# Sums of squares of three heads and of one norm as two fp32r matmuls; one table set for the last two heads' factors

## The reference

```
def rmsnorm(x, gain):
    y = x * rsqrt(mean(x * x, axis=-1) + 1e-6)
    return y * gain

o = rmsnorm(o, out_gain)            # per head, over its 128 values
o = o * silu(g)
return o.reshape(B, S, H * V) @ w_out
```

```
x = x + (silu(g) * u) @ w_down
gate = sigmoid(rmsnorm(x, g_ple) @ w_ple_gate)
x = x + gate * (p_i @ w_ple)
```

## Time and profile before

| | us |
|---|---|
| median of 3 runs | 2105.17 |
| lowest, highest | 2104.57, 2105.2 |
| the profiled execution, its own time | 2104.74 |
| its span in the trace | 2102.3 |
| PE busy | 2092.1 |
| POOL busy | 1143.1 |
| DVE busy | 1008.4 |
| ACT busy | 742.9 |

### The profile page before, as it was taken

How to read it: one execution, slowest core, us unless ns; L and a number is a source line. 1 busy time by engine, 2 the same in 40 slices (tenths; PEclk the granted TensorE clock), 3 DMA queues, 4 the chain that set the end, 5 groups by cost and what they waited for, 6 DMA issues and landing times.

```text
span 2102.3 us, 28240 instructions
## 1 busy us (share of the span) xinstructions
PE 2092.1 (100%) x11210; PEld 1738.5 (83%) x11210; DVE 1008.4 (48%) x1184; ACT 742.9 (35%) x862; POOL 1143.1 (54%) x821
## 2 busy tenths in 40 slices
PE   9999999999999999999999999999999999999998
PEld 8888888888888888888888888888888888888887
DVE  6357555555123265634555333744477544453126
ACT  6335542222224445533222233515433332212234
POOL 6677455555555333365555555544566555555553
PEclk9999999999999999999999999999999999999999
DMA  5212132222232222242222222322222222223321
GB/s 199 81 62 82 41 120 100 85 95 100 100 119 96 96 67 94 81 138 95 88 98 100 100 100 100 102 98 101 99 88 94 99 100 100 100 88 105 117 100 60
DMA packets 33209, 204.39 MB, mean 97 GB/s; under 512 B 3688, under 2 KB 6504, under 8 KB 9456
## 3 DMA queue, kind: packets, MB, share of 16 engines
q1 hardware_dynamic: 32896, 203.13, 28.1%
q10 hardware_dynamic: 240, 0.23, 0.0%
HBM read 200.19 MB, written 2.10 MB: 96 GB/s over the span
## 4 chain that ended last, share of the span: by engine, by line
PE 58%; DVE 1%; ACT 1%; issue 0%; DVEq 0%; ACTq 0%
PE bank L1952 58%; DVE x L1835 0%; DVE sgate L1884 0%; ACT w_hi L775 0%; DVE h L1885 0%; PE bank L2363 0%; DVE ssq L1909 0%; ACT sgate L775 0%; DVE h L1931 0%; ACT un L775 0%; ACT L1289 0%; ACT L1286 0%; ACT L1282 0%; ACT L1279 0%; ACT sq L775 0%
## 5 line engine op out<-in xcount | busy, mean ns | idle before, releaser
L652 POOL TENSOR_TENSOR w_lo<-raw,w_hi 128x512 fp32r<-128x512 f32 x676 | 976.6, 1475 | 862.2 <-ACT w_hi L775 862.2
L1952 PE MATMUL bank<-u_hi,w_hi 128*128 128x512 f32 (+1 forms) x1936 | 753.5, 390 | 0.1
L1952 PE MATMUL bank<-u_lo,w_hi 128*128 128x512 f32 (+1 forms) x1936 | 749.4, 387 | 0.0
L775 ACT ACTIVATE w_hi<-raw 128x2048 fp32r<-128x2048 f32 x185 | 354.3, 1915 | 931.4 <-PE bank L1952 927.8
L1952 PE MATMUL bank<-u_hi,w_lo 128*128 128x512 f32 (+1 forms) x1936 | 482.1, 387 | 0.0
L1952 PEld LDWEIGHTS bank<-u_hi,w_hi 128*128 128x128 f32 x1936 | 363.6, 188 | 74.6 <-ACTq L1185 0.5
L1952 PEld LDWEIGHTS bank<-u_lo,w_hi 128*128 128x128 f32 x1936 | 363.7, 188 | 73.7 <-issue 0.2
L1952 PEld LDWEIGHTS bank<-u_hi,w_lo 128*128 128x128 f32 x1936 | 362.5, 188 | 74.6
L1952 PE MATMUL bank<-act_hi,w_hi 128*128 128x512 f32 x528 | 205.4, 389 | 0.0
L1952 PE MATMUL bank<-act_lo,w_hi 128*128 128x512 f32 x528 | 205.4, 389 | 0.0
L1324 DVE TENSOR_TENSOR h<-h,bank 128x512 f32<-128x512 f32 x48 | 30.8, 683 | 300.3 <-PE bank L1952 300.3
(11 more groups left out here) (293 smaller groups left out, 2105.5 us busy)
## 6 DMA issues: line engine op xcount, KB each, us to landing
raw<-wall SPq DMA_DIRECT2D x185, 1024.0 KB, 4.9
out_t<-h SPq DMA_DIRECT2D x8, 256.0 KB, 2.5
h<-x_t SPq DMA_DIRECT2D x3, 512.0 KB, 7.3
first_raw<-wall SPq DMA_DIRECT2D x6, 256.0 KB, 7.5
av_moved<-av SPq DMA_DIRECT2D x14, 64.0 KB, 2.1
h<-x_t SPq DMA_DIRECT2D x2, 256.0 KB, 3.4
first_raw<-wall SPq DMA_DIRECT2D x4, 128.0 KB, 3.8
lmask_f<-lmask_in SPq DMA_DIRECT2D x1, 512.0 KB
```

The costliest lines, as they stand in the source:

```text
L652: ins = nc.gpsimd.tensor_tensor(w_lo[:, s, c], raw[:, s, c], w_hi[:, s, c].bitcast(F32), ALU.subtract)
L775: return nc.scalar.activation(out, in_, func, **k)
L1952: return nc.tensor.matmul(out, lhsT, rhs, start=start, stop=stop, skip_group_check=True)
```

## The change

The sums of heads 5, 6 and 7 and of norm 6 are split like the others: a copy on ACT, a subtraction, and two fp32r matmuls for one float32 matmul. The low part of head 5 is made by POOL, between `fold_keys(3, 6)` and the panel piece; those of heads 6 and 7 by DVE (`last_squares_lower`), each behind its `head_taken`. That of norm 6 is made by DVE, as for norms 1 to 5, and its high part by ACT ahead of the copies to `side`. PE's `mean_squares(6)` moves one `out_step` forward, `mean_squares(7)` one back. ACT loads the table set that holds both logarithm and exponential ahead of head 7's square, and makes the factor and the high part of head 6 before those of head 7. DVE finishes head 6 before head 7. `SPLIT_HEADS` is now only the number of the head from which the step `root_log` and `mean_squares` of a tail are taken in order, and is called `LATE_HEADS`.

```diff
@@ pool, pair 3
                         if l == 3:
                             head_lower(2 * p - 2)
+                        if l == 6:
+                            head_lower(2 * p - 1)
                         if l in (3, 4):
                             out_pieces(HOUT, 2 * l - 6, 2 * l - 4)
                         elif l == 6:
                             out_pieces(HOUT + 1, 0, 1)
@@ act, residual
-                if m < 6:
+                if m < 7:
                     upper_sums(m)
@@ act, head_squares
                 af(sq[:, hd % 2, :], tail_bank(hd)[:], ACT.Square).then_inc(osq_ready, 1)
-                if hd < SPLIT_HEADS:
-                    act.wait_ge(osq_ready, hd + 1)
-                    if hd:
-                        act.wait_ge(oms_done, hd)
-                    af(sum_hi[1][:], sq[:, hd % 2, :], ACT.Copy).then_inc(osq_upper, 1)
+                act.wait_ge(osq_ready, hd + 1)
+                if hd:
+                    act.wait_ge(oms_done, hd)
+                af(sum_hi[1][:], sq[:, hd % 2, :], ACT.Copy).then_inc(osq_upper, 1)
@@ act, behind the pairs
             head_squares(HG - 2)
+            nc.scalar.preload_act_table_set("natural_log_exp_and_others")
             head_squares(HG - 1)
-            root_log(HG - 2)
-            root_log(HG - 1)
-            root_exp(HG - 2)
-            root_exp(HG - 1)
-            head_upper(HG - 2)
-            head_upper(HG - 1)
+            for hd in (HG - 2, HG - 1):
+                root_log(hd)
+                root_exp(hd)
+                head_upper(hd)
@@ dve, residual
-                for a in range(0 if m == 6 else 2 if m == TWIN else 1):
+                for a in range(2 if m == TWIN else 1):
@@ dve, new
+            def last_squares_lower(hd):
+
+                dve.wait_ge(osq_upper, hd + 1)
+                tt(sum_lo[1][:], sq[:, hd % 2, :], sum_hi[1][:].bitcast(F32), ALU.subtract).then_inc(osq_split, 1)
@@ dve, behind the pairs
-            head_taken(HG - 2)
-            head_taken(HG - 1)
-            last_made(HG - 2)
-            last_made(HG - 1)
-            last_lower(HG - 2)
-            last_lower(HG - 1)
+            for hd in (HG - 2, HG - 1):
+                head_taken(hd)
+                last_squares_lower(hd)
+            for hd in (HG - 2, HG - 1):
+                last_made(hd)
+                last_lower(hd)
@@ pe, norm
-                if 0 < m < 6:
+                if 0 < m < 7:
@@ pe, mean_squares
-                if hd < SPLIT_HEADS:
-                    pe.wait_ge(osq_split, hd + 1)
-                    mm(root_bank(hd)[:], ones_r[:], sum_hi[1][:], True, False)
-                    mm(root_bank(hd)[:], ones_r[:], sum_lo[1][:], False, True).then_inc(oms_done, 1)
-                else:
-                    pe.wait_ge(osq_ready, hd + 1)
-                    mm(root_bank(hd)[:], ones[:], sq[:, hd % 2, :]).then_inc(oms_done, 1)
+                pe.wait_ge(osq_split, hd + 1)
+                mm(root_bank(hd)[:], ones_r[:], sum_hi[1][:], True, False)
+                mm(root_bank(hd)[:], ones_r[:], sum_lo[1][:], False, True).then_inc(oms_done, 1)
@@ pe, behind the pairs
             outputs(HG - 1)
+            mean_squares(HG - 2)
             out_step(HOUT + 1, 2)
-            mean_squares(HG - 2)
+            out_step(HOUT + 1, 3)
             mean_squares(HG - 1)
-            out_step(HOUT + 1, 3)
             out_step(HOUT + 1, 4)
```

More of the change, by code:

```diff
@@ L112 @@
 HOUT = len(MIX)
-SPLIT_HEADS = 5
+LATE_HEADS = 5
 LEVEL_SLICES = ((3,) * 8, (3,) * 8, (3, 3, 2, 3, 2, 3, 2, 2), (2, 2, 3, 3, 2, 2, 1, 1))
@@ L972, in tail @@
                     head_squares(hd)
-                elif step == 3 and hd >= SPLIT_HEADS:
+                elif step == 3 and hd >= LATE_HEADS:
                     root_log(hd)
@@ L2266, in tail @@
                     outputs(hd)
-                elif hd >= SPLIT_HEADS:
+                elif hd >= LATE_HEADS:
                     mean_squares(hd)
```

## The result

The changed kernel took 2107.8 us (median of 22 runs, 2106.49 to 2109.38), the kernel before 2104.98 us beside it (22 runs, 2104.01 to 2106.54). The ratio is 1.0014, with a 95% interval of 1.0008 to 1.002: slower by 2.8 us, clear of the noise, and within the 0.2% that the prediction counts as the same. The forecast was 2107.3 us. The profiled execution took 2106.68 us with a span of 2104.5; before it was 2104.74 and 2102.3. Three executions on record, one of the kernel with both places mended and two of the kernel before, ran at a mean clock of 0.85 or lower and count in no ratio here.

What follows compares the result with a forecast made beforehand. PE bounds the kernel, busy 2092.1 of 2102.3 us. Terms 1.05 - 0.79 + 2.3 - 0.41 = +2.15 us on 2105.17 gave 2107.3 us, with a range of 2105.0 to 2109.6.

Steps and rivals of the forecast that it cites:

- The sums: Split sums on PE save 0.41 us at norm 6, 0.79 at heads 6 and 7, 0.41 at head 5.
- Norm 6: At the side input: PE waits 2.3 us for ACT's side copies behind the copy, less 0.41 us gained: +1.9 us.
- Heads 6 and 7: Operands ready in time, so no wait; 0.79 us gained on PE, leaving +0.26 us from the transposes on.
- the whole gain that the change can have on PE: All four split sums together: 0.41 + 0.79 + 0.41 = 1.61 us off PE.
- the best case of 2103.6 us: No wait at the side copies or at head 5, so the full 1.61 us is gained.
- Head 5: PE waits 0.9 us for POOL's low part, then half a us at the transposes: 1.05 us later, 0.41 us gain included.
- The clock: Rival, 20%: the clock falls in the wait at the side input, costing 1.5 us more: 2108.8 us, 2110.4 at most.
- a bound of 3.05 us: Most that a low clock stretch could cost, from the kernel's start, where it lasts to at most 7.1 us.
- The tail's figure: In the trace's tail the clock fell 1.2 to 1.7 us after PE's last matmuls, less than the forecast wait.
- The side copies do hold PE: Rival denied this at group 3: 2105.0 us; 12% together with the waits at head 5 being hidden.
- The set serves: Rival, 3%: the table set fails, four loads of 1.28 us follow head 7's copy, 3.5 us more: 2110.8 us.
- The dearer switch: A skill page's 2.66 us per table switch on ACT, making the table set rival about 5.5 us worse still.

Runs made afterwards that it cites:

- both places mended: Changed kernel with norm 6's high part behind the side copies of groups 0 and 1, and head 5's low part behind POOL's panel piece: 2104.06 us against 2104.5.
- the third experiment: Changed kernel with norm 6's high part made on ACT behind the side copies of groups 0 and 1 instead of ahead: 2104.53 us against 2104.5.
- the first experiment: Changed kernel with norm 6 as one float32 matmul again, heads 5 to 7 still split: 2105.45 us, ratio 1.0005.
- the last experiment: Changed kernel, norm 6's high part behind side copies of groups 0 and 1, head 5's low part behind POOL's last key product: 2103.92 us against 2104.62.

## Why the prediction was right

The sign, the mechanism and the places were right, and the sum was close. Point by point, in distances within the traces so that the start does not enter (the changed kernel's trace stands 0.16 us earlier at the level products of l = 7):

- *The sums.* Norm 6 is worth what was worked out: the third experiment gained 0.4 us there. Heads 6 and 7 gave 0.74 of 0.79 us. That head 5's float32 sum costs 0.41 us more on PE is right as a distance, but the prediction took it for gain: "the whole gain that the change can have on PE", 1.61 us, was too large by at least that 0.41 us, and with it the best case of 2103.6 us for a kernel whose waits are all gone by reordering. The two runs that tried this show 0.3 us from the heads, where the terms of the sum make 1.20 us; leaving head 5 alone gave 0.74. In the sum for this change it did no harm, since POOL's wait covers DVE's.
- *Head 5.* Waits of 0.9 and 0.5 us were forecast, 0.79 and 0.55 came. The transposes stand 0.98 + 0.16 = 1.14 us later, where 1.05 was forecast. POOL's steps took 1.27, 1.29 and 1.50 us for 1.45, 1.40 and 1.05; the errors have both signs, so that the sum of the three is 4.06 us for 3.90.
- *Heads 6 and 7.* No wait, as forecast. From the level products to DVE's first addition + 0.38 us, for + 0.26.
- *Norm 6.* ACT's and PE's order is that of the prediction. PE would have started group 3 at 2041.43 + 0.23 = 2041.66 and did at 2043.85: 2.2 us, for 2.3, of which 2.04 are booked as waiting. The span is 2.2 us longer in all, for 2.15.
- *The clock.* This is the step whose weight was off. The rival had 20%; it was in fact 10 of the 22 executions. Its price, taken as 1.5 us, measured 1.5 to 1.8, and that agreement is luck: 1.5 was half of a bound of 3.05 us, with part of the low stretch thought to lie in the wait. In all four falls that are traced (one at 2.0 us and one at 3.6 us at the side input, two without the table set) the clock was 1.00 through the wait and fell only once the matmuls had begun again, so that nothing of the price was hidden. The tail's figure of 1.2 to 1.7 us from PE's last matmul to the fall did not carry over either: in the trace of the changed kernel PE stands for 2.04 us and the clock does not fall. The forecast of 2107.3 lies between the two groups, 2107.0 and 2108.8, and so does the median of 2107.8. The two numbers agree within 0.5 us partly for that reason, and partly because the forecast started from a median of 2105.17 us of three runs, where 22 runs gave 2104.98: as a difference from before, 2.15 us were forecast and 2.8 measured, 2.0 in the lower group. Had the clock fallen in a few more runs, the median would have been near 2108.8 at the same mechanism. That PE is full on both sides of the wait, which I had put against the rival, did not protect it.
- *The other rivals.* The side copies do hold PE (third experiment). The set serves, and without it the wait is there: 3.58 us, near the 3.5 us that follow from the trace's 1.28 us for a load. The dearer switch that the prediction quotes beside it would have made it about 9 us, so the measurement decides for the load's own 1.28 us.

What remains open: why the clock falls in some executions and not in others after the same 2.0 us; and up to 0.6 us between the traces and the medians of some runs (the first experiment: 0.4 us longer in the trace, 0.95 by the median), which is within their intervals.

## What to carry to other kernels

When the bound engine is full, a cheaper operation on it pays only if its operands are ready as early as before; here each split put two more steps, on engines that work in order, ahead of PE, and what was queued behind the waiting step cost more (2.04 us for the side copies, 0.55 us for the key product) than the 0.41 us that the split saved. Look first at what a new wait is placed in front of: moving one copy behind four others took the median from 2.8 us above that of before to equal with it, the falls of the clock included. And before counting the time of an instruction as gain, ask what else is late at its end: head 5's long sum had been hiding DVE's copy.

## What the runs showed of the hardware

A standstill of the matmul engine can cost more than its own length. By the mean clock of each execution, the granted clock fell from 2.4 to 1.2 GHz after 2.0 us without a matmul in 15 of 33 executions, after 3.6 us in 8 of 8, after 1.1 us in none of 11. In the four falls that are traced it came 0.8, 0.7 and 0.6 us after the matmuls had begun again, and once with the first of them (worked out from the mean clock of the us in which it fell: 0.91, 0.91, 0.81 and 0.81), and the wait itself was at 1.00; it cost about 1.6 us through matmuls 0.43 us apart for 0.23. Eight small matmuls whose result nobody uses, put into the wait, kept it up in 11 of 11 runs.

VectorE's last query product took 0.69 us where POOL's key product had begun 0.93 us ahead of it (before, and in the last experiment), 1.21 us where it had begun 0.40 us ahead (both places mended), and 1.42 us in the changed kernel, where it began 0.83 us behind, and a panel piece was running instead. In all four traces the product ended 0.55 to 0.57 us behind the end of the POOL instruction that was running when it began, whichever that was. The reverse shows too: POOL's subtraction that began 0.08 us behind VectorE's product took 1.74 us, for 1.27 us in the changed kernel. So a shift of a few tenths of a us between these two engines can double the duration of an instruction on one of them. The ends of POOL's instructions in a trace are rough, and no run isolates the pair.
